# Local attention of a two-layer block: values as zero-padded blocks, one multiply out of PSUM, gating by inverse sums on GpSimd

## The chip, the core and the metric

The kernel runs on one core of a Trainium2 chip. The metric is the time of one execution on the device in microseconds (us). Five queues of instructions run side by side: TensorE (PE, with its weight loads shown as PEld), VectorE (DVE), ScalarE (ACT), GpSimd (POOL) and the DMA issues of SyncE (SP). Each works through its own program in order; they meet at semaphores.

## The reference, cut to what matters

The whole program is two blocks: an even mixer, an odd mixer, and a second block with a gated feed-forward part. The change lies in the odd mixer, an attention over a window of keys with a sink, 1024 tokens, 16 query heads in 4 groups of 4 that share one key and value head, head size 64:

```python
def windowed_sink_attention(q, k, v, sink, slopes):
    ...                                   # a block of 128 queries sees its own 128 keys and those on either side
    sc = jnp.einsum('bnqkgd,bnskd->bnkgqs', qb, kb).astype(jnp.float32) * scale + bias
    m = jnp.maximum(jnp.max(sc, axis=-1, keepdims=True), sink_l)
    p = jnp.exp(sc - m)
    denom = jnp.sum(p, axis=-1, keepdims=True) + jnp.exp(sink_l - m)
    o = jnp.einsum('bnkgqs,bnskd->bnqkgd', (p / denom).astype(v.dtype), vb)

def odd_mixer(h, w_in, sink, w_out, slopes):
    qc, kc, vc, gc = jnp.split(h @ w_in, [C_Q, C_Q + C_KV, C_Q + 2 * C_KV], axis=-1)
    oc = windowed_sink_attention(...)
    return (oc * jax.nn.silu(gc)) @ w_out
```

Products are made from two rounded parts of each operand, a high one and a low one (the rest after rounding), so that a product takes three matrix products: high by high, low by high, high by low.

## The kernel before, in words

The odd mixer is three stages: projection (`*_odd_proj`), the local attention (`*_attention_c`), output projection (`*_odd_out`). The attention walks over 32 groups g, each one key head i = g // 8 and one block of 128 queries n = g % 8. A group has four query heads and is done as two units u = 2g and u = 2g + 1 of two heads each. A block sees three blocks of keys, at the two ends of the sequence (n = 0 and n = 7) two.

Each engine has a loop over u written by hand, and the order in it is the order of execution. In the step of unit u:

- PE: scores of u (`pe_c_scores`, six matmuls into PSUM banks 0 and 1, in pairs on two halves of the array); transposes of the exponentials of u - 1 (`pe_c_turn`, two or three for each head); in odd steps `pe_c_spread`, two transposes of the inverse sums into bank 7; in even steps `pe_c_values` of group u / 2 - 2 into bank 6.
- DVE: `dve_c_bias` twice (adds the bias to the scores out of PSUM and takes the row's extreme), `dve_c_low` of u - 2 (the low part of the transposed exponentials); in even steps the inverse of the sums first, and `dve_c_gate` last; in odd steps `dve_c_add` last.
- ACT: `act_c_raise` twice (exponentials with their sums), `act_c_high` of u - 1 (the high part out of PSUM); in even steps `act_c_move`. In steps 5, 7 and 9 of each key head but the last it also makes the high parts of the next head's keys (`act_c_keys`) and queries (`act_c_query`).
- POOL: in even steps `pool_c_wide` (spreads the inverse sums over 64 columns for a head), in odd steps `pool_c_mix`, and in between the low parts of the next head's keys, queries and values and its bias tables. `c_pool_in_turn` makes every POOL operation wait for the one before it.

Scores of unit u wait for the biases of u - 1, since banks 0 and 1 are there once. Transposes of u - 1 wait for the exponentials of u - 1 (`c_raised`) and for the low parts of u - 3 (`c_low`), which free their banks. The values of a group wait for its low parts and for the last reader of bank 6 in the group before.

Before, the weights of the value product are 128 columns, 64 of the high part of V and 64 of its low part (`C_VS`), and the moving operand is all four heads, 512 columns, once with the high exponentials (`C_PTH`) and once with the low ones (`C_PTL`): 2 matmuls for each block of keys, 4 or 6 for a group. Bank 6 then holds two sums in its two halves of 64 rows. ACT moves the lower half to the upper rows (`C_OT`), DVE adds the two in two pieces of 64 x 256 (`C_O2`), and POOL multiplies by `C_G`. That was made by DVE from bank 7 (the inverse sums, transposed) and the gate in `MIX`. The product goes back into `MIX`, which the output projection reads.

Of the kernel before, what the change touches and what calls it, by code (L numbers as in the profile page):

```python
# [14 lines left out]
P = 128  # L15
# [107 lines left out]
def build(nc, d, where, known):  # L123
# [1401 lines left out]
    def act_odd_proj():  # L1525
# [42 lines left out]
    def dve_odd_proj():  # L1568
# [57 lines left out]
    c_biased, c_low, c_inverse, c_gated, c_added, c_key_low0, c_query_low0, c_sinks = signal("c_dve").steps(
        "biased", "low", "inverse", "gated", "added", "key_low0", "query_low0", "sinks")
    c_raised, c_high, c_moved, c_key_high, c_query_high, c_sink = signal("c_act").steps(
        "raised", "high", "moved", "key_high", "query_high", "sink")
# [56 lines left out]
    def pe_c_values(g):  # L1686
# [61 lines left out]
    def dve_c_gate(g):  # L1748
        i, n = g // TT, g % TT
        dve.wait_ge(*c_spread.at(g))  # L1750
        if g >= 2:
            dve.wait_ge(*c_mixed.at(g - 2))
        dve.tensor_tensor(C_G[:, g % 2, :].rearrange("p (t n) -> p t n", t=2),
                          ps[:, 7, 0:2 * P].rearrange("p (t n) -> p t n", t=2), mix_pair(i, n),
                          ALU.mult).then_inc(*c_gated.up(g))

    def dve_c_add(g):
        dve.wait_ge(*c_moved.at(g))
        if g >= 2:
            dve.wait_ge(*c_mixed.at(g - 2))  # L1760
        for e in range(2):
            high, low = (x.rearrange("p (t e n) -> p e t n", t=2, e=2)[:, e]
                         for x in (ps[0:HD, 6, :], C_OT[0:HD, :]))
            last = dve.tensor_tensor(C_O2[g % 2][rows(e, HD), :].rearrange("p (t n) -> p t n", t=2), high, low, ALU.add)
        last.then_inc(*c_added.up(g))
# [16 lines left out]
    def act_c_keys(i):  # L1782
        base = (i % 2) * HD
        for r in range(2):
            act.activation(C_KH[rows(r, HD), i, :], KC[base:base + HD, i // 2, :], ACT.Copy).then_inc(*c_key_high.up(i, r))

    def act_c_query(t):
        if t >= 4:
            act.wait_ge(*c_scored.at(2 * (8 * (t // 2 - 2) + 7) + t % 2, 1))
        else:  # L1790
            act.wait_ge(*vc_turned.at(1))
# [25 lines left out]
    def act_c_move(g):  # L1817
        act.wait_ge(*c_summed.at(g))
        act.activation(C_OT[0:HD, :], ps[HD:P, 6, :], ACT.Copy).then_inc(*c_moved.up(g))

    def act_attention_c():
        act.wait_ge(*w_used.at(ODD_PROJ[-1]))
        for u in range(NU + 5):
# [10 lines left out]
            i = u // 16 + 1  # L1834
            if i < C_KV:
                if u % 16 == 5:
                    act_c_keys(i)
                elif u % 16 in (7, 9):
                    act_c_query(2 * i + (u % 16 - 7) // 2)
            elif u % 16 == 5 and u < NU:  # L1840
                act_high(ODD_OUT[0])

    def pool_c_values(i):
        v = C_VS[:, i % 2, :, :]
# [3 lines left out]
        pool.tensor_copy(v[:, :, 0:HD], VC[:, :, rows(i, HD)]).then_inc(*c_v_high.up(i))  # L1848
# [1245 lines left out]
```

## Time and profile before

| | us |
|---|---|
| median of 3 runs (2415.68 to 2421.56) | 2418.89 |
| the profiled execution | 2413.29 |
| its span, from first to last instruction | 2412.0 |

| engine | busy us | share of the span |
|---|---|---|
| PE | 2322.6 | 96% |
| PEld | 1925.3 | 80% |
| DVE | 1394.3 | 58% |
| ACT | 1133.5 | 47% |
| POOL | 929.8 | 39% |

The local attention takes the time from 1060 to 1237 us of the span, 7% of it. Shares over the whole span tell nothing of this stage, in which other engines do far more than on average; it has to be read by its own window. PE's busy time counts each matmul up to its modelled end, so that a stage with PE 90% busy can still hold waits and overlaps: for PE the starts of instructions are the better guide.

### The profile page before, as it was taken

Reading aid. Unit: us, or ns where it says so; the run is one execution under the profiler, and the core shown is the slowest. Engines: PE = TensorE matmul, PEld = TensorE weight load, DVE = VectorE, ACT = ScalarE, POOL = GpSimd, SP = SyncE. Lnnn points to the kernel's source line nnn. Section 1 sums busy time; section 2 is a strip of 40 time slices with the busy share of each in tenths; the row PEclk is TensorE's granted clock in tenths of the full one; section 3 lists DMA queues with packets and bytes.
Section 4 is the critical chain, followed back from the end, with each engine's and each line's share of the span. In section 5 each row is a group of like instructions: output and inputs, shape, how many; then the busy total and the mean of one; then the engine's idle time right before and its main releaser. Section 6 shows DMA issues by size and latency. Waiting matters only on the chain.

```text
span 2412.0 us, 31494 instructions
## 1 busy us (share of the span) xinstructions
PE 2322.6 (96%) x12074; PEld 1925.3 (80%) x12074; DVE 1394.3 (58%) x1899; ACT 1133.5 (47%) x1796; POOL 929.8 (39%) x711
## 2 busy tenths in 40 slices
PE   5999999989999999998999999999999999999998
PEld 5888789868888888876678777788877888888887
DVE  6256599768884330139973743332676666666665
ACT  5322488778883221249952474232333333333334
POOL 1112256436652212335521112122265555555551
PEclk8999999999999999999999999999999999999999
DMA  8265200010003121100021121122211111111111
GB/s 307 76 166 177 76 6 1 4 33 1 1 1 122 67 95 44 53 1 1 10 105 44 60 95 44 36 83 66 71 31 52 55 55 54 53 53 53 53 53 70
DMA packets 154089, 146.46 MB, mean 61 GB/s; under 512 B 12294, under 2 KB 141364, under 8 KB 152020
## 3 DMA queue, kind: packets, MB, share of 16 engines
q1 hardware_dynamic: 153940, 144.45, 19.2%
q8 instruction: 96, 1.57, 0.3%
q14 instruction: 53, 0.43, 0.1%
HBM read 123.85 MB, written 16.78 MB: 58 GB/s over the span
## 4 chain that ended last, share of the span: by engine, by line
PE 80%; ACT 6%; issue 5%; DVE 4%; POOL 2%; DMA 1%; SPq 1%; ACTq 0%; DVEq 0%; POOLq 0%
PE ps L256 37%; PE ps L2650 15%; PE ps L2667 9%; PE ps L1127 5%; PE ps L1150 4%; PE ps L1137 4%; ACT C_PR L1807 1%; PE ps L1696 1%; POOL WSL L2567 1%; ACT B_PR L1211 1%; ACT B_PTH L1205 1%; PE ps L2626 1%; ACT C_PTH L1815 1%; PE ps L1675 1%; POOL WSR L2549 1%
## 5 line engine op out<-in xcount | busy, mean ns | idle before, releaser
L243 POOL TENSOR_TENSOR WL<-WR,WH 128x1024 fp32r<-128x1024 f32 (+2 forms) x87 | 203.0, 2334 | 764.8 <-ACT WH L238 764.6
L256 PE MATMUL ps<-HH,WH 128*128 128x512 f32 (+2 forms) x1136 | 358.8, 397 | 0.0
L256 PE MATMUL ps<-HL,WH 128*128 128x512 f32 (+2 forms) x1136 | 351.7, 391 | 0.0
L256 PE MATMUL ps<-HH,WL 128*128 128x512 f32 x1104 | 341.8, 391 | 0.0
L256 PEld LDWEIGHTS ps<-HL,WH 128*128 128x128 f32 (+2 forms) x1136 | 212.1, 187 | 47.7
L256 PEld LDWEIGHTS ps<-HH,WH 128*128 128x128 f32 (+2 forms) x1136 | 208.4, 187 | 47.1 <-issue 4.1
L256 PEld LDWEIGHTS ps<-HH,WL 128*128 128x128 f32 x1104 | 208.1, 188 | 44.0
L2880 DVE TENSOR_TENSOR XF<-ps,XF 128x1024 f32<-128x1024 f32 x168 | 201.5, 1220 | 33.0 <-PE ps L2667 26.4
L2650 PE MATMUL ps<-HC,WSH 128*128 128x512 f32 x640 | 197.0, 389 | 0.0
L1163 DVE TENSOR_REDUCE NM<-ps 128x1 f32<-128x1024 f32 x128 | 156.6, 1223 | 35.9 <-PE ps L1127 34.4
L2567 POOL TENSOR_TENSOR WSL<-WSR,WSH 128x512 fp32r<-128x512 f32 x100 | 131.5, 1315 | 107.5 <-ACT WSH L2561 107.5
L2561 ACT ACTIVATE WSH<-WSR 128x512 fp32r<-128x512 f32 x100 | 62.9, 629 | 220.2 <-POOL WSR L2549 220.2
L2549 POOL TENSOR_TENSOR WSR<-WS 128x512 f32<-128x512 f32 x100 | 133.9, 1339 | 36.3 <-PE ps L2650 36.3
L2650 PE MATMUL ps<-HS,WSH 128*128 128x512 f32 x480 | 147.7, 389 | 0.0
L2650 PEld LDWEIGHTS ps<-HC,WSH 128*128 128x128 f32 x640 | 120.1, 188 | 24.9
L2650 PE MATMUL ps<-HC,WSL 128*128 128x512 f32 x320 | 124.6, 389 | 0.0
L2667 PE MATMUL ps<-AH,OWH 128*128 128x512 f32 x352 | 110.0, 394 | 6.5 <-DVE XF L2880 4.4
L2567 POOL TENSOR_TENSOR WSL<-WS,WSH 128x512 fp32r<-128x512 f32 x48 | 65.0, 1356 | 125.7 <-ACT WSH L2561 125.7
L2839 DVE TENSOR_TENSOR CG<-CG,ps 128x512 f32<-128x512 f32 x60 | 41.3, 688 | 119.2 <-ACT CG L2728 89.4
L2667 PE MATMUL ps<-AH,OWL 128*128 128x512 f32 x352 | 108.7, 390 | 0.0
L2667 PE MATMUL ps<-AL,OWH 128*128 128x512 f32 x352 | 108.6, 390 | 0.0
L1726 DVE CUSTOM_DVE_ANT_0 C_SB<-ps,BF,NSINK 128x384 f32<-128x384 f32 (+1 forms) x128 | 68.9, 576 | 67.1 <-POOL C_VS L1848 60.3
(433 smaller groups left out, 5183.0 us busy)
## 6 DMA issues: line engine op xcount, KB each, us to landing
WS<-in_w_ffn_in SPq DMA_DIRECT2D x44, 512.0 KB, 5.0
MKW<-in_ada_w SPq DMA_DIRECT2D x32, 512.0 KB, 3.9
spill<-X SPq DMA_DIRECT2D x3, 4096.0 KB, 13.6
OW<-in_w_ffn_out SPq DMA_DIRECT2D x22, 512.0 KB, 3.5
WR<-in_odd_w_in SPq DMA_DIRECT2D x19, 512.0 KB, 3.7
WR<-in_w_in SPq DMA_DIRECT2D x19, 512.0 KB, 3.7
WR<-in_even_w_in SPq DMA_DIRECT2D x17, 512.0 KB, 5.5
AWK<-in_ada_w SPq DMA_DIRECT2D x8, 1024.0 KB, 9.4
```

The lines of the kernel that those rows point to most:

```text
L243: pool.tensor_tensor(low[:, :, :], raw[:, :, :], high[:, :, :].bitcast(F32), ALU.subtract).then_inc(*w_low.up(t))
L256: last = pe.matmul(ps[0:w.out, 2 * s + h, :], wt[:, k, :], x[:, k, halves(h)], start=(k == 0 and n == 0), stop=(k == w.kt - 1 and n == len ...
L1127: last = pe.matmul(ps[:, b + j, :], qs[:, rows(q)], ks[:, halves(j)], start=(n == 0), stop=(n == len(passes) - 1))
L1137: last = pe.transpose(ps[:, 4 + j, rows(k)], D.PR[:, p % 3, rows(4 * j + k)], IDENT[:, :])
L1150: last = pe.matmul(ps[:, 6 + pg % 2, 0:2 * P], D.VS[D.v_of(h)][:, k, :], pt[pg % 2][:, k, :], start=(k == 0 and n == 0), stop=(k == TT - 1 ...
L1163: dve.tensor_reduce(NM[:, s % 4:s % 4 + 1], pair(2 * (s % 2)), AX_X, ALU.max, negate=True).then_inc(*m_done.up(g, s))
L1726: dve.tensor_tensor_reduce(C_SB[:, hd, WIN - w:WIN], ps[:, j, 0:w], BF[i % 2][:, hd, b0:b0 + w], -1.0, NSINK[:, 4 * i + hd:4 * i + hd + 1] ...
L2549: pool.tensor_tensor(WSR[:, q % RING, :, :], w_block(*a), w_block(*b), op).then_inc(*ws_sum.up(q))
L2567: pool.tensor_tensor(WSL[:, q % RING, :, :], src, WSH[:, q % RING, :, :].bitcast(F32), ALU.subtract).then_inc(*ws_low.up(q))
L2650: last = pe.matmul(ps[:, BANK[o], :], w[:, q % RING, k, :], OPERAND[o][:, x, k, :], start=(k == 0 and n == 0), stop=(k == HK - 1 and n == 2))
L2667: done = pe.matmul(ps[:, 4 + 2 * (n % 2) + h, :], w[:, rows(n)], x[:, halves(h)], start=(first and m == 0), stop=(last and m == 2))
L2880: dve.tensor_tensor(LAST.x[:, n, :], pair(4 + 2 * (n % 2)), LAST.x[:, n, :], ALU.add).then_inc(*y_added.up(r, n))
```

## The change

The value product writes its result where it is wanted. `C_VS` becomes five blocks of 64 columns for each block of keys: zero, V high, zero, V low, zero. A slice of 128 columns that starts at a zero block puts its product in one half of the rows and zeros in the other; two such slices (e = 0 and 1) put the two heads of a pair into the two halves of bank 6. There are three terms (high by high, low by high, high by low) with two slices each, of 256 columns: 6 matmuls for each block of keys, 12 or 18 for a group. `C_PTH` and `C_PTL` hold the heads in another order for this.

With that the move of a half (`C_OT`) and the two additions are gone. ACT copies the transposed inverse sums from bank 7 to `C_G` instead (`act_c_move`), POOL multiplies them there by the gate in `MIX` (`pool_c_gate`), and DVE multiplies bank 6 by `C_G` into `MIX` (`dve_c_mix`). The high parts of the next head's keys and queries go from ACT to POOL (`pool_c_next_keys`, `pool_c_next_query`), and POOL clears the zero blocks (`pool_c_clear`: buffer 0 at the start, buffer 1 in step 5). The output projection waits for `c_mixed` instead of `c_added`.

```diff
     def pe_c_spread(g):
         pe.wait_ge(*c_wide.at(g))
         if g:
-            pe.wait_ge(*c_gated.at(g - 1))
+            pe.wait_ge(*c_moved.at(g - 1))
...
         if g:
-            pe.wait_ge(*c_added.at(g - 1))
-        for k in range(hi - lo):
-            for m, pt in enumerate((C_PTH, C_PTL)):
-                last = pe.matmul(ps[:, 6, :], C_VS[:, i % 2, lo + k, :], pt[:, g % 2, k, :, :].rearrange("p h n -> p (h n)"),
-                                 start=(k == 0 and m == 0), stop=(k == hi - lo - 1 and m == 1))
+            pe.wait_ge(*c_mixed.at(g - 1))
+        v = C_VS[i % 2][:, :, :, :].rearrange("p t b n -> p t (b n)")
+        nk = hi - lo
+        for k in range(nk):
+            for m, (c0, pt) in enumerate(((0, C_PTH), (2, C_PTH), (0, C_PTL))):
+                for e in range(2):
+                    a = HD * (c0 + 1 - e)
+                    last = pe.matmul(ps[:, 6, 0:2 * P], v[:, lo + k, a:a + P], pt[:, g % 2, k, e, :, :].rearrange("p t n -> p (t n)"),
+                                     start=(k == 0 and m == 0 and e == 0), stop=(k == nk - 1 and m == 2 and e == 1))
...
-    def dve_c_gate(g):
...
-    def dve_c_add(g):
...
+    def dve_c_mix(g):
         i, n = g // TT, g % TT
+        dve.wait_ge(*c_gated.at(g))
+        dve.wait_ge(*c_summed.at(g))
+        dve.tensor_tensor(mix_pair(i, n), ps[:, 6, 0:2 * P].rearrange("p (t n) -> p t n", t=2),
+                          C_G[:, g % 2, :].rearrange("p (t n) -> p t n", t=2), ALU.mult).then_inc(*c_mixed.up(g))
...
-            if u % 2 == 0 and 4 <= u < NU + 4:
-                dve_c_gate((u - 4) // 2)
             if u % 2 == 1 and 5 <= u < NU + 5:
-                dve_c_add((u - 5) // 2)
+                dve_c_mix((u - 5) // 2)
...
     def act_c_move(g):
-        act.wait_ge(*c_summed.at(g))
-        act.activation(C_OT[0:HD, :], ps[HD:P, 6, :], ACT.Copy).then_inc(*c_moved.up(g))
+        act.wait_ge(*c_spread.at(g))
+        if g >= 2:
+            act.wait_ge(*c_mixed.at(g - 2))
+        act.activation(C_G[:, g % 2, :], ps[:, 7, 0:2 * P], ACT.Copy).then_inc(*c_moved.up(g))
...
-            i = u // 16 + 1
-            if i < C_KV:
-                if u % 16 == 5:
-                    act_c_keys(i)
-                elif u % 16 in (7, 9):
-                    act_c_query(2 * i + (u % 16 - 7) // 2)
...
+    def pool_c_clear(b):
+        for block in (0, 2, 4):
+            c_pool_in_turn()
+            pool.memset(C_VS[b][:, :, block, :].bitcast(F32), 0.0).then_inc(*c_v_clear.up(b, block))
...
+    def pool_c_next_keys(i):
+        base = (i % 2) * HD
+        for r in range(2):
+            c_pool_in_turn()
+            pool.tensor_copy(C_KH[rows(r, HD), i, :], KC[base:base + HD, i // 2, :]).then_inc(*c_next_key.up(i, r))
+
+    def pool_c_next_query(t):
+        if t >= 4:
+            pool.wait_ge(*c_scored.at(2 * (8 * (t // 2 - 2) + 7) + t % 2, 1))
+        c_pool_in_turn()
+        pool.tensor_copy(C_QH[t % 4][:, :], QC[:, t, :]).then_inc(*c_next_query.up(t))
...
-    def pool_c_mix(g):
+    def pool_c_gate(g):
...
+        g_ = C_G[:, g % 2, :].rearrange("p (t n) -> p t n", t=2)
+        pool.tensor_tensor(g_, g_, mix_pair(i, n), ALU.mult).then_inc(*c_gated.up(g))
...
             if u % 2 == 0 and 2 <= u <= NU:
                 pool_c_wide((u - 2) // 2)
-            if u % 2 == 1 and 5 <= u < NU + 5:
-                pool_c_mix((u - 5) // 2)
+            if u % 2 == 0 and 4 <= u < NU + 4:
+                pool_c_gate((u - 4) // 2)
+            if u == 5:
+                pool_c_clear(1)
...
+                elif u % 16 == 5:
+                    pool_c_next_keys(i)
                 elif u % 16 == 6:
                     pool_c_keys(i)
+                elif u % 16 in (7, 9):
+                    pool_c_next_query(2 * i + (u % 16 - 7) // 2)
...
     def pe_odd_out():
         pe_stay_awake(7, 0)
-        pe.wait_ge(*c_added.at(NG - 1))
+        pe.wait_ge(*c_mixed.at(NG - 1))
```

On PE, in an even step of a middle block, this is what stood between the scores of one unit and those of the next (L1662 scores, L1675 transposes, L1696 values):

```order
L1662 MATMUL ps<-C_KL_180,C_QH_184 128x384 x2
L1675 MATMUL ps<-IDENT,C_PR 128x128 x6
L1696 MATMUL ps<-C_PTH,C_VS 128x512
L1696 MATMUL ps<-C_PTL,C_VS 128x512
L1696 MATMUL ps<-C_PTH,C_VS 128x512
L1696 MATMUL ps<-C_PTL,C_VS 128x512
L1696 MATMUL ps<-C_PTH,C_VS 128x512
L1696 MATMUL ps<-C_PTL,C_VS 128x512
L1662 MATMUL ps<-C_KH,C_QH_185 128x384 x2
```

The same place on PE in the changed kernel (its lines are 1661, 1674 and 1699):

```order
L1661 MATMUL ps<-C_KL_180,C_QH_184 128x384 x2
L1674 MATMUL ps<-IDENT,C_PR 128x128 x6
L1699 MATMUL ps<-C_PTH,C_VS_188 128x256 x4
L1699 MATMUL ps<-C_PTL,C_VS_188 128x256 x2
L1699 MATMUL ps<-C_PTH,C_VS_188 128x256 x4
L1699 MATMUL ps<-C_PTL,C_VS_188 128x256 x2
L1699 MATMUL ps<-C_PTH,C_VS_188 128x256 x4
L1699 MATMUL ps<-C_PTL,C_VS_188 128x256 x2
L1661 MATMUL ps<-C_KH,C_QH_185 128x384 x2
```

Nothing moved on PE: the value product stands where it stood, with 18 matmuls of 256 columns for 6 of 512.

On POOL, in steps 4 to 10 of the first key head, the order before (L1857 bias table, L1887 mix, L1879 wide, L1865 low part of keys, L1871 of queries):

```order
L1857 TENSOR_SCALAR BF_200<-AWAY,SLOPE 128x384
L1887 TENSOR_TENSOR MIX<-C_O_194,C_G 128x2x128
L1879 COPY C_RID<-C_RI 128x256
L1865 TENSOR_TENSOR C_KL_181<-KC,C_KH 64x1024 x2
L1887 TENSOR_TENSOR MIX<-C_O_195,C_G 128x2x128
L1879 COPY C_RID<-C_RI 128x256
L1871 TENSOR_TENSOR C_QL<-QC,C_QH_186 128x1024
L1887 TENSOR_TENSOR MIX<-C_O_194,C_G 128x2x128
L1879 COPY C_RID<-C_RI 128x256
L1871 TENSOR_TENSOR C_QL<-QC,C_QH_187 128x1024
```

The same steps on POOL in the changed kernel (L1883 gate, L1827 clear, L1857 and L1863 the copies that came from ACT):

```order
L1843 TENSOR_SCALAR BF_198<-AWAY,SLOPE 128x384
L1827 MEMSET C_VS_189 128x8x64 x3
L1857 CAST C_KH<-KC 64x1024 x2
L1875 COPY C_RID<-C_RI 128x256
L1883 TENSOR_TENSOR C_G<-C_G,MIX 128x256
L1850 TENSOR_TENSOR C_KL_181<-KC,C_KH 64x1024 x2
L1863 CAST C_QH_186<-QC 128x1024
L1875 COPY C_RID<-C_RI 128x256
L1883 TENSOR_TENSOR C_G<-C_G,MIX 128x256
L1867 TENSOR_TENSOR C_QL<-QC,C_QH_186 128x1024
L1863 CAST C_QH_187<-QC 128x1024
L1875 COPY C_RID<-C_RI 128x256
```

The copies stand ahead of the wide steps, and the multiply by the gate has moved from behind the additions of the odd step to the even step, right behind the wide step of the next group.

## Rows read from the trace of the kernel before

**Rows 1.** Busy time in the local attention's window: PE, PEld, DVE, ACT, POOL, clock, DMA

```profile
1060.00:1237.00 177.00, 156.67 (x1009) 112.81 (x1008) 159.51 (x449) 158.53 (x374) 89.87 (x97) 1.00 0.02 6
```

**Rows 2.** Timeline of one group: start, length, engine, line, operation, idle before and releaser

```profile
1208.68 0.45 PE L1662 MATMUL ps<-C_KH,C_QH 64*128 64x384 f32 x2
...
1209.51 0.62 DVE L1726 CUSTOM_DVE_ANT_0 C_SB<-ps,BF,NSINK 128x384 f32<-128x384 f32 x1 [0.23 <-PE ps L1662]
...
1210.43 0.48 PEld L1662 LDWEIGHTS ps<-C_KH,C_QH 64*128 64x128 f32 x2 [0.17 <-issue]
...
1210.59 0.95 DVE L1740 TENSOR_TENSOR C_PTL<-ps,C_PTH 128x768 fp32r<-128x768 f32 x1
...
1211.66 0.64 PEld L1675 LDWEIGHTS ps<-IDENT,C_PR 128*128 128x128 f32 x6 [0.46 <-ACT C_PR L1807]
...
1212.44 0.47 PE L1696 MATMUL ps<-C_PTH,C_VS 128*128 128x512 f32 x1
...
1213.66 0.39 PE L1696 MATMUL ps<-C_PTL,C_VS 128*128 128x512 f32 x1
...
1213.97 0.44 PE L1662 MATMUL ps<-C_KH,C_QH 64*128 64x384 f32 x2
```

**Rows 3.** Groups by shape in the same window: count, busy us, mean ns, idle before

```profile
L1696 PE MATMUL ps<-C_PTH,C_VS 128*128 128x512 f32 x88 | 37.0, 421 | 2.1 <-DVE C_O L1764 1.4
```

**Rows 4.** Timeline of an earlier attention's value product, eight matmuls of 256 columns

```profile
395.76 0.36 PE L1150 MATMUL ps<-A_PTH,A_VS 128*128 128x256 f32 x1
...
395.96 0.28 PE L1150 MATMUL ps<-A_PTL,A_VS 128*128 128x256 f32 x1
...
396.68 0.28 PE L1150 MATMUL ps<-A_PTL,A_VS 128*128 128x256 f32 x1
```

**Rows 5.** Timeline of PE: first scores of five odd units

```profile
1118.54 0.44 PE L1662 MATMUL ps<-C_KH,C_QH 64*128 64x384 f32 x2
...
1136.23 0.45 PE L1662 MATMUL ps<-C_KH,C_QH 64*128 64x384 f32 x2
...
1160.78 0.44 PE L1662 MATMUL ps<-C_KH,C_QH 64*128 64x384 f32 x2
...
1178.62 0.44 PE L1662 MATMUL ps<-C_KH,C_QH 64*128 64x384 f32 x2
...
1224.60 0.39 PE L1662 MATMUL ps<-C_KH,C_QH 64*128 64x256 f32 x2
```

**Rows 6.** Groups by shape, as Rows 3: what is removed, added or moved

```profile
L1764 DVE TENSOR_TENSOR C_O<-ps,C_OT 64x256 f32<-64x256 f32 x64 | 26.4, 412 | 2.7 <-ACT C_OT L1819 2.2
L1819 ACT ACTIVATE C_OT<-ps 64x512 f32<-64x512 f32 x32 | 19.0, 595 | 4.1 <-PE ps L1696 3.4
L1887 POOL TENSOR_TENSOR MIX<-C_O,C_G 128x256 f32<-128x256 f32 x24 | 17.7, 739 | 44.6 <-DVE C_O L1764 44.2
L1871 POOL TENSOR_TENSOR C_QL<-QC,C_QH 128x1024 fp32r<-128x1024 f32 x6 | 14.3, 2388 | 1.2 <-ACT C_PR L1807 0.4
L1879 POOL COPY C_RID<-C_RI 128x256 f32<-128x256 f32 x32 | 12.8, 398 | 7.6 <-POOL MIX L1887 3.2 <-DVE C_RI L1746 2.8 <-POOL GATE L1887 0.9
L1753 DVE TENSOR_TENSOR C_G<-ps,MIX 128x256 f32<-128x256 f32 x24 | 10.0, 415 | 0.0
L1792 ACT ACTIVATE C_QH<-QC 128x1024 fp32r<-128x1024 f32 x6 | 6.3, 1053 | 0.0
L1848 POOL CAST C_VS<-VC 128x512 fp32r<-128x512 f32 x4 | 2.5, 616 | 17.7 <-PE ps L256 17.4
```

**Rows 7.** Waits in the same window: who waited for whom, us, times, longest

```profile
PEld ps L1696 <- DVE C_O L1764: 3.8, 8, 1.6
```

**Rows 8.** Timeline of the attention's end

```profile
1231.21 0.47 PE L1696 MATMUL ps<-C_PTH,C_VS 128*128 128x512 f32 x1 [1.44 <-DVE C_O L1764]
...
1232.41 0.59 ACT L1819 ACTIVATE C_OT<-ps 64x512 f32<-64x512 f32 x1 [2.23 <-PE ps L1696]
...
1234.72 3.90 ACT L435 ACTIVATE HH<-MIX 128x1024 fp32r<-128x1024 f32 x4 [1.72 <-POOL GATE L1887]
```

More of the change, by code:

```diff
@@ L1620, in build @@
-    C_OT, C_O2 = place("C_OT", 139.53125, [P, HALF]), [place("C_O20", 141.53125, [P, 2 * P]), place("C_O21", 117.75, [P, 2 * P])]
+    C_KL = [place(f"C_KL{i}", kb, [P, SEQ], F32R) for i, kb in enumerate((107.5, 149.5, 153.5, 157.5))]
+    C_QH = [place(f"C_QH{i}", kb, [P, SEQ], F32R) for i, kb in enumerate((51, 55, 161.5, 165.5))]
+    C_VS = [place("C_VS0", 117.5, [P, TT, 5, HD], F32R), place("C_VS1", 169.5, [P, TT, 5, HD], F32R)]
+    C_PTH, C_PTL = place("C_PTH", 179.5, [P, 2, 3, 2, 2, P], F32R), place("C_PTL", 191.5, [P, 2, 3, 2, 2, P], F32R)
@@ L1624, in build @@
     c_tables = signal("c_tables")
     c_scored, c_turned, c_spread, c_summed = signal("c_scored"), signal("c_turned"), signal("c_spread"), signal("c_summed")
[L1626 to L1629, printed above, removed]
+    c_biased, c_low, c_inverse, c_mixed, c_key_low0, c_query_low0, c_sinks = signal("c_dve").steps(
+        "biased", "low", "inverse", "mixed", "key_low0", "query_low0", "sinks")
@@ L1630, in build @@
+    c_raised, c_high, c_key_high, c_query_high, c_sink, c_moved = signal("c_act").steps(
+        "raised", "high", "key_high", "query_high", "sink", "moved")
     c_pool = signal("c_pool")
-    c_mixed, c_wide, c_bias, c_v_high, c_values, c_key_low, c_query_low = c_pool.steps(
-        "mixed", "wide", "bias", "v_high", "values", "key_low", "query_low")
+    c_wide, c_gated, c_bias, c_v_clear, c_v_high, c_values, c_next_key, c_next_query, c_key_low, c_query_low = c_pool.steps(
+        "wide", "gated", "bias", "v_clear", "v_high", "values", "next_key", "next_query", "key_low", "query_low")
@@ L1746, in dve_c_inverse @@
         dve.reciprocal(C_RI[:, g % 2, :], C_RS[:, g % 2, :]).then_inc(*c_inverse.up(g))
-    def dve_c_gate(g):
+    def dve_c_mix(g):
         i, n = g // TT, g % TT
[L1750 to L1755, printed above, removed]
-    def dve_c_add(g):
[L1758 to L1765, printed above, removed]
+        dve.wait_ge(*c_gated.at(g))
+        dve.wait_ge(*c_summed.at(g))
+        dve.tensor_tensor(mix_pair(i, n), ps[:, 6, 0:2 * P].rearrange("p (t n) -> p t n", t=2),
+                          C_G[:, g % 2, :].rearrange("p (t n) -> p t n", t=2), ALU.mult).then_inc(*c_mixed.up(g))
     def dve_attention_c():
@@ L1776, in dve_attention_c, with act_c_keys @@
                 dve_c_low(u - 2)
-            if u % 2 == 0 and 4 <= u < NU + 4:
-                dve_c_gate((u - 4) // 2)
             if u % 2 == 1 and 5 <= u < NU + 5:
-                dve_c_add((u - 5) // 2)
-    def act_c_keys(i):
-        base = (i % 2) * HD
+                dve_c_mix((u - 5) // 2)
+    def act_c_keys():
         for r in range(2):
-            act.activation(C_KH[rows(r, HD), i, :], KC[base:base + HD, i // 2, :], ACT.Copy).then_inc(*c_key_high.up(i, r))
+            act.activation(C_KH[rows(r, HD), 0, :], KC[0:HD, 0, :], ACT.Copy).then_inc(*c_key_high.up(0, r))
     def act_c_query(t):
[L1788 to L1791, printed above, removed]
+        act.wait_ge(*vc_turned.at(1))
         act.activation(C_QH[t % 4][:, :], QC[:, t, :], ACT.Copy).then_inc(*c_query_high.up(t))
@@ L1847, in pool_c_values @@
         c_pool_in_turn()
[L1848 removed]
+        pool.tensor_copy(v[:, :, 1, :], VC[:, :, rows(i, HD)]).then_inc(*c_v_high.up(i))
         c_pool_in_turn()
[L1850 removed]
+        pool.tensor_tensor(v[:, :, 3, :], VC[:, :, rows(i, HD)], v[:, :, 1, :].bitcast(F32),
                            ALU.subtract).then_inc(*c_values.up(i))
@@ L1880, in pool_c_wide @@
                          C_RI[:, g % 2, :].unsqueeze(2).to_broadcast([P, 4, HD])).then_inc(*c_wide.up(g))
-    def pool_c_mix(g):
+    def pool_c_gate(g):
         i, n = g // TT, g % TT
-        mix = mix_pair(i, n)
-        pool.wait_ge(*c_added.at(g))
+        pool.wait_ge(*c_moved.at(g))
         c_pool_in_turn()
-        pool.tensor_tensor(mix, C_O2[g % 2][:, :].rearrange("p (t n) -> p t n", t=2),
-                           C_G[:, g % 2, :].rearrange("p (t n) -> p t n", t=2), ALU.mult).then_inc(*c_mixed.up(g))
+        g_ = C_G[:, g % 2, :].rearrange("p (t n) -> p t n", t=2)
+        pool.tensor_tensor(g_, g_, mix_pair(i, n), ALU.mult).then_inc(*c_gated.up(g))
     def pool_attention_c():
```

20 lines of the change are left out of this document (7 added, 13 removed).

## The prediction

> **What bounds the kernel now.** The change touches one stage, so I read that stage by its own window first. There three engines stand level: of 177 us PE is busy for 156.7, DVE for 159.5, ACT for 158.5, POOL for half of that, and the granted clock is 1.00, the level of 2.4 GHz [rows 1]. Busy shares so close together don't say which engine sets the pace; a loop of waits can. So the next view is the timeline of one group in the middle of a key head, and the reader is to follow from the scores of one odd unit to the scores of the next odd unit [rows 2]:
>
> - Scores start at 1208.68. DVE had been idle for 0.23 when they released its first bias at 1209.51: it follows the scores and isn't late. The two biases end where the low part begins, 1210.59.
> - The transposes of that unit need its exponentials (ACT, behind the biases) and the low part that stands behind the biases on DVE, 1210.59 + 0.95 = 1211.54. They start at 1211.66, after PE's loads had been idle for 0.46 [rows 2]. From the scores that is 2.98.
> - Transposes take up to 1212.44, 0.78. Then the value product, six matmuls, the last at 1213.66; the next odd scores follow it at 1213.97, 1.53 after the first.
>
> 2.98 + 0.78 + 1.53 = 5.29, and that is the measured distance of the two odd scores. So the pace is a loop through PE, DVE, ACT and PE again, in which **the value product stands in line** with the two biases and the low part. The additions, the gate multiply and the move are not in it: they run while the loop is elsewhere. Three such periods in an undisturbed stretch are 1224.60 - 1208.68 = 15.92, 5.31 each [rows 2, 5].
>
> I take the sum against the profiled execution, 2413.29 (span 2412.0 and 1.3 around it). It lies 5.6 below the median of the runs, 2418.89, and the forecast is the median plus the change.
>
> **The change part by part.**
>
> *The value product, in the loop.* 88 blocks of keys (88 matmuls with the high part [rows 3], as many with the low) have 2 matmuls of 512 columns each and get 6 of 256. In the middle of a product the starts of 512-column matmuls lie (1213.66 - 1212.44) / 5 = 0.244 apart with the first one's delay, about 0.229 without it (the first takes some 0.08 more, as 0.20 against 0.12 in [rows 4]). For 256 columns with 128 x 128 weights the trace has the same form in an earlier attention, with a new weight load each time: 395.96 to 396.68 are six steps of 0.12 [rows 4]. A group of three key blocks goes from 6 x 0.229 = 1.37 to 18 x 0.12 = 2.16, **+0.79**; one of two blocks from 0.92 to 1.44, **+0.52**. There are 24 of the one and 8 of the other: 24 x 0.79 + 8 x 0.52 = **+23.1**. Nothing covers it, since the next scores wait in PE's queue behind it and the biases wait for them.
>
> The Trainium skill, "TensorE: Matmul & The Clock Gate", section "Back-to-back issue gap", gives a warm gap of N / 2.4 + 2.5 ns. By it 256 columns would take 0.109 and 512 take 0.216, and the term would be an estimated 24 x 0.67 + 8 x 0.45 = 19.7 instead of 23.1. The rows show a little more for both widths, and I keep the rows.
>
> *Additions, gate, mix on DVE.* Two additions of 0.412 go for each group, and one multiply out of PSUM replaces another of the same shape (0.415) [rows 6]. DVE loses 64 x 0.412 = 26.4 busy us, but in the loop it works only at the biases and the low part, which stay: worth nothing there. Only where PE has fewer transposes (four instead of six) do the additions come late for the next values. Seven such waits are left of [rows 7] beside the one of 1.6 at the end: 2.2 together, with the usual gap of a load in it; **-1.5**. The new multiply stands behind the same low part, 0.415 instead of 0.82 long, and doesn't wait there: its gate was made a group before.
>
> *ACT's move.* 64 x 512 (0.595) becomes 128 x 256, half the columns; between nothing and 0.595 a group, off the loop. It now waits for the spread instead of the sum, and the next exponentials queue behind it; the spread stands one step earlier on PE, so I cost it at nothing. If it did hold ACT, its slack before the next transposes is the long value product.
>
> *Keys and queries from ACT to POOL.* Four ACT operations of some 1.05 a head [rows 6] go from steps 5 to 9. What they cost now is read from odd scores three periods apart: 1136.23 - 1118.54 = 17.69 and 1178.62 - 1160.78 = 17.84 [rows 5] against 15.92. That is 1.77 and 1.92; the first head is taken like these: 3 x 1.84 = **-5.5**.
>
> On POOL they are new work. A copy with rounding takes 0.616 for 512 columns, so 1.23 for 1024; the other bound is the two-operand form with 2.39 [rows 6]. I take 1.23, the same operation. Between the wide steps of groups 2 and 3 of a head POOL then has 0.40 + 0.74 + 2 x 2.39 + 1.23 = 7.15, and five gaps between operations of up to 0.24 (7.6 idle ahead of 32 wide steps [rows 6]), so 7.2 to 8.4, against a new period of 5.30 + 0.79 = 6.09. The spread on PE can be late by 0 to 2.3 a head, in the first head by three clears of 0.40 to 0.62 more (copy and cast [rows 6] as bounds): 0 to 8.8 in all. Most is absorbed, since the inverse sums are ready nearly a period before the spread stands at the head of PE's queue: half a microsecond a head, **+1.5**.
>
> *The end.* There is no cover there. PE waited 1.44 for the last additions but one [rows 8]; without move and additions, 0.595 + 0.82, but with a multiply of 0.415, it waits 1.0 less. From the last sums to the output projection's first operation on ACT were 1234.72 - 1232.41 = 2.31 [rows 8], move, additions and POOL's 0.74; a multiply of 0.415 and a hand-over remain, about 0.5: 1.8 less. **-2.8**. The waits of output projection and its loads hang on `c_mixed` before and after, and shift with it.
>
> Sum: 23.1 - 1.5 - 5.5 + 1.5 - 2.8 = **+14.8**: 2413.29 becomes 2428.1, and the median 2418.89 becomes **2433.7**.
>
> **The rivals.**
>
> *The relieved engines set the pace (not slower).* If the waits in the loop went away with the lighter DVE and ACT, only PE's own work would count. Of the 5.29 PE waited 0.46 ahead of the transposes and about 0.29 ahead of the second even scores (a pair of loads that takes 0.48 and not 0.19 [rows 2]). 5.29 - 0.75 + 0.79 = 5.33 a period, as much as now, and what remains are the -1.5, -5.5 and -2.8: 2418.89 - 9.8 + 32 x 0.03 = 2410. It decides from the point where the first bias no longer starts with the scores' end. For it speaks DVE's 90% [rows 1]; against it the 0.23 in which DVE stood idle for the scores. The Trainium skill, "Perfetto Trace Analysis", section "Optimizing Scalar/DVE Operations", says that offloading a saturated DVE to ScalarE or GpSimd may make sense; by that rule this is the likely case, and the idle time in the loop is what the trace says against it. Chance 0.10.
>
> *POOL becomes the bound in steps 5 to 10 (slower still).* There it has three times 0.40 + 0.74, four copies of 1.23 and four low parts of 2.39, 17.9, with 14 gaps up to 21.3, in three periods of 6.09 = 18.3; up to 3.0 too much, which its lead absorbs. Were the copies at the two-operand price, 4 x 1.16 = 4.6 more, a head would lose up to 7.6 and three heads 23 instead of the 1.5: +36 at most, 2455. Against it: the cast in this stage's rows is cheap [rows 6]. Chance 0.12, mostly in part of that size.
>
> *The value product is hidden after all.* PE's waits could lie elsewhere in other groups, so that the longer product fills them; with 0.46 of each 0.79 hidden the sum is +14.8 - 32 x 0.44 = about +1, 2420. Against it: the wait ahead of the transposes starts at the odd scores, which move with the product. Chance 0.08.
>
> **How the numbers follow.** The forecast has 0.70, its own range 2427 to 2441 (skill's gaps below; POOL's term at 8.8 above). The range for 8 in 10 takes in most of the third case and the nearer half of the POOL case: 2420 to 2446. Within 0.2%, 4.8 us, a measurement of this kernel can't tell a change from none. Slower: 0.70 + 0.12 and little of the rest, 0.82. Faster: 0.09 of the first rival. Same: 0.09.
>
> **What would show it.** Right: 256-column value matmuls 0.12 apart; odd scores 6.1 apart in the middle of a head where it was 5.3; DVE near 159.5 - 26.4 = 133 busy us in the stage and ACT near 140 (158.5 less twelve operations of 1.05 and part of the move), both with idle time; PE's wait ahead of the transposes still there, released by ACT or the low part; the last sums within 0.6 of the output projection. Wrong: odd scores 5.3 to 5.4 apart (first rival); PE's scores or transposes waiting for POOL's spread, or DVE's multiply for POOL's gate, by over a microsecond a head (second); a transposes' wait shrunk to nothing (third).

## The result and the profile after

The changed kernel takes 2427.29 us in the median against 2420.22 of the kernel before beside it, a ratio of 1.0035 with an interval of 1.0024 to 1.0046: 6 to 11 us slower, where +14.8 was forecast (2433.7, range 2420 to 2446). Direction and range hold; the forecast change is half as large again as the +9.7 that the stage shows (next paragraph) and lies above the interval.

The stage, from its first scores to the first matmul of the output projection, was 177.0 (1060.15 to 1237.16) and is 186.7 (1067.03 to 1253.69): **+9.7**. The profiled run began it 6.9 later, after a wait for weights some 800 us earlier and a stretch at a granted clock of 0.50 (6.8 us) right behind that wait, which the change doesn't touch, and was 2.9 shorter behind the stage; I compare within the stage. Busy time there, with the columns of [rows 1]:

```profile
1067.00:1253.70 186.70, 175.47 (x1362) 146.24 (x1361) 133.90 (x386) 136.50 (x362) 105.33 (x115) 1.00 0.02 7
```

DVE has lost 26 us of work and ACT 22, as meant, and the stage is longer: PE's busy time has gone up by 19. One group of the timeline answers to [rows 2]:

```profile
1218.94 0.44 PE L1661 MATMUL ps<-C_KH,C_QH 64*128 64x384 f32 x2
...
1219.77 0.62 DVE L1729 CUSTOM_DVE_ANT_0 C_SB<-ps,BF,NSINK 128x384 f32<-128x384 f32 x1 [1.56 <-PE ps L1661]
...
1221.72 0.41 DVE L1755 TENSOR_TENSOR GATE<-ps,C_G 128x256 f32<-128x256 f32 x1
1221.92 0.64 PEld L1674 LDWEIGHTS ps<-IDENT,C_PR 128*128 128x128 f32 x6 [0.46 <-ACT C_PR L1792]
...
1222.55 0.72 PE L1699 MATMUL ps<-C_PTH,C_VS 128*128 128x256 f32 x4
...
1223.35 0.64 PE L1699 MATMUL ps<-C_PTH,C_VS 128*128 128x256 f32 x4
...
1224.07 0.64 PE L1699 MATMUL ps<-C_PTH,C_VS 128*128 128x256 f32 x4
...
1224.88 0.44 PE L1661 MATMUL ps<-C_KH,C_QH 64*128 64x384 f32 x2
```

Odd scores to odd scores: 5.94, where it was 5.29. Scores to transposes is 2.98 as before, with the same 0.46 of waiting for the exponentials. The product takes 2.33 for 1.53 (1223.35 to 1224.07 is six matmuls, 0.12 each). Between them stand 0.63 from transposes to product, where 0.78 stood. DVE waits 1.56 for the scores instead of 0.23: it idles longer in a longer loop.

What was added and moved, by shape as [rows 6]: DVE's multiply, ACT's copy, POOL's gate, wide step and one of the copies.

```profile
L1755 DVE TENSOR_TENSOR MIX<-ps,C_G 128x256 f32<-128x256 f32 x24 | 10.0, 415 | 1.4 <-POOL C_G L1883 1.4
L1806 ACT ACTIVATE C_G<-ps 128x256 f32<-128x256 f32 x32 | 11.8, 368 | 1.5 <-PE ps L1682 1.5
L1883 POOL TENSOR_TENSOR C_G<-C_G,MIX 128x256 f32<-128x256 f32 x24 | 17.6, 732 | 29.2 <-ACT C_G L1806 27.9 <-POOL C_RID L1875 0.4
L1875 POOL COPY C_RID<-C_RI 128x256 f32<-128x256 f32 x32 | 12.7, 398 | 26.8 <-DVE C_RI L1749 24.4 <-POOL C_QH L1863 0.8 <-POOL C_KH L1857 0.5
L1863 POOL CAST C_QH<-QC 128x1024 fp32r<-128x1024 f32 x6 | 6.2, 1038 | 0.7
```

The new waits are nearly all idle time of engines off the loop. The end, to be read against [rows 8]:

```profile
1249.97 0.40 PE L1699 MATMUL ps<-C_PTL,C_VS 128*128 128x256 f32 x2
1250.21 3.73 PE L368 MATMUL ps<-IDENT 128*128 128x128 f32 x32
1250.47 0.42 DVE L1755 TENSOR_TENSOR GATE<-ps,C_G 128x256 f32<-128x256 f32 x1 [1.92 <-PE ps L1699]
...
1250.93 5.79 ACT L435 ACTIVATE HH<-MIX 128x1024 fp32r<-128x1024 f32 x6 [2.27 <-DVE GATE L1755]
...
1253.69 0.70 PE L256 MATMUL ps<-HH,ODD_FIRST 128*128 128x512 f32 x2
```

One multiply stands between the last sums and the output projection's first operation: 0.56 from the modelled end of the sums (1249.97 + 0.40 = 1250.37) to 1250.93, where 2.31 stood. What comes last there now is PE's own filler (L368, matmuls without a use with which `pe_stay_awake` fills the wait; 1253.69 follows them without a gap).

### The profile page after: what moved, and what is told of

Read it like the earlier page. It is cut to its first block, busy times and chain, and to the rows that moved or that the text cites. A ratio compares the mean times of both kernels' runs of the same rounds, so it can differ in the third digit from the quotient of the medians.

```text
span 2425.6 us, 32135 instructions
## 1 busy us (share of the span) xinstructions
PE 2342.9 (97%) x12426; PEld 1959.5 (81%) x12426; DVE 1367.1 (56%) x1835; ACT 1110.3 (46%) x1784; POOL 947.0 (39%) x729
## 4 chain that ended last, share of the span: by engine, by line
PE 82%; DVE 5%; ACT 4%; issue 4%; POOL 2%; DMA 2%; SPq 1%; DVEq 0%; ACTq 0%; POOLq 0%
PE ps L256 35%; PE ps L2652 15%; PE ps L2669 9%; PE ps L1127 5%; PE ps L1150 4%; PE ps L1137 4%; PE ps L1699 2%; DMA MKW<-in_ada_w 1%; PE ps L1661 1%; PE ps L1674 1%; ACT B_PR L1211 1%; ACT B_PTH L1205 1%; PE ps L2628 1%; DMA WR<-in_w_in 1%; DVE MKA L525 1%
```

## The experiments

Theory: the pace is the loop of [rows 2], and the product stands in line. Open were where 5 us of the forecast went, and what ACT's relief is worth in a shorter loop. A period is the time from the scores of one odd unit to those of the next. Besides the ratio to the kernel before I give the time from the third odd scores (unit 5) to the first matmul of the output projection, since in most of the profiled runs (not in before, after and e1) PE's clock fell at the start of the stage. Windows of e14_before_spread (columns as [rows 1]):

```profile
1066.00:1071.50 5.50, 3.18 (x26) 2.13 (x24) 2.42 (x10) 4.95 (x12) 4.72 (x6) 0.99 0.00 0
1071.50:1077.50 6.00, 6.00 (x26) 4.30 (x25) 3.98 (x14) 3.84 (x11) 3.91 (x4) 0.50 0.01 4
```

After a stretch in which PE was busy for 3.18 of 5.5, the granted clock was 0.50 (1.2 GHz) for 6 us; that costs about 2.4 us ahead of the third odd scores (13.3 from the first scores to them, 10.9 in before).

| kernel | ratio to before, 95% | third odd scores to output projection, us |
|---|---|---|
| before | 1 | 166.1 |
| after | 1.0035 [1.0024, 1.0046] | 175.3 |
| e13_before_one_addition | 0.9966 [0.9953, 0.9978] | 160.7 |
| e2_mix_halves | 1.0072 [1.0055, 1.0089] | 181.6 |
| e1_two_terms | 0.9979 [0.9967, 0.9991] | 164.3 |
| e3_copies_on_act | 1.0042 [1.0026, 1.0058] | 176.0 |
| e6_clear_later | 1.0034 [1.0023, 1.0045] | 173.8 |
| e5_before_pool_copies | 1.0032 [1.0022, 1.0041] | 171.9 |
| e14_before_spread | 0.9970 [0.9959, 0.9981] | 161.6 |
| e9_before_split | 1.0102 [1.0084, 1.0120] | 188.4 |
| e8_split_product | 1.0009 [1.0000, 1.0019] | 167.8 |
| e10_split_clear | 1.0000 [0.9990, 1.0010] | 165.4 |
| e11_split_act_copies | 1.0016 [1.0003, 1.0029] | 167.1 |
| e12_split_spread | 0.9983 [0.9973, 0.9993] | 160.8 |

**What did the additions cost?** First the changed kernel with its multiply as slow as the two additions:

```diff
+        for e in range(2):
+            r = rows(e, HD)
+            last = dve.tensor_tensor(mix_pair(i, n)[r], ps[r, 6, 0:2 * P].rearrange("p (t n) -> p t n", t=2),
+                                     C_G[r, g % 2, :].rearrange("p (t n) -> p t n", t=2), ALU.mult)
+        last.then_inc(*c_mixed.up(g))
```

> The changed kernel with VectorE's multiply in two pieces of 64 rows, as long (0.83) as the two additions that it replaced and in the same place. Theory A: in the kernel before, the next product waited for the additions in every group (0.15 in the middle, 0.36 where four transposes stand ahead), and the change took that wait away; then it comes back here: 24 x 0.15 + 8 x 0.36 = 6.5 us slower than the changed kernel, transposes to product 0.78 again instead of 0.63. Rival B: the forecast's 1.5 for this wait was right and the forecast was off elsewhere; then +1 to +2 us.

It is 6.3 longer from the third odd scores on, 0.9 of it at the end, behind the last odd scores: the theory's size. Then the kernel before with one addition fewer:

```diff
-        for e in range(2):
+        for e in range(2 if g < 2 else 1):
```

> The kernel before, with the second of the two additions of a group left out from the third group on (so heads' odd halves of the result aren't brought up to date: that part of the computation is missing). The additions' end then comes 0.42 us earlier, and nothing else of the product or of ScalarE changes. In the trace of before the product began 0.14 to 0.15 us after the second addition's end in 18 of 32 groups, and there it stood 0.75 us behind its transposes with six of them and 0.67 to 0.72 with four, against 0.63 and about 0.4 in the changed kernel. Theory (the additions held the product in these groups, and the loop of odd scores passes through that): 11 x 0.12 + 3 x 0.33 + 4 x 0.26 = 3.4 us less in the stage (177.0 to 173.6), middle odd scores of the last head 5.15 to 5.2 instead of 5.29 to 5.32, time about 3.5 below before (ratio 0.9985). Rival (the prediction's size): 1.5 us less, odd scores at 5.29, ratio 0.9994.

It is 5.4 shorter by the same measure, 1.2 of it at the end, which the expectation had left out; middle odd scores of the last head lie 5.17 to 5.18 apart, as the theory said, those around a change of heads 4.52, 3.85 and 4.65 where they were 4.88, 4.15 and 4.91. DVE's last operation on the sums, from the timelines, in before (its product starts at 1212.44 [rows 2]), e2 and e13:

```profile
1211.46 0.83 DVE L1764 TENSOR_TENSOR C_O<-ps,C_OT 64x256 f32<-64x256 f32 x2
```

```profile
1228.11 0.85 DVE L1757 TENSOR_TENSOR GATE<-ps,C_G 64x256 f32<-64x256 f32 x2
...
1229.11 0.59 PE L1699 MATMUL ps<-C_PTH,C_VS 128*128 128x256 f32 x3
```

```profile
1216.03 0.41 DVE L1764 TENSOR_TENSOR C_O<-ps,C_OT 64x256 f32<-64x256 f32 x1
...
1216.86 0.47 PE L1696 MATMUL ps<-C_PTH,C_VS 128*128 128x512 f32 x1
```

From DVE's end to the product: 0.15 in before and e2, 0.42 in e13 and in after (1221.72 + 0.41 to 1222.55). Over all groups it is 0.14 to 0.15 in 18 of 32 before, 0.14 to 0.16 in nearly every group of e2, and in after 0.19 or more but for the last group. So a constant 0.15 marks the groups in which the product waited for DVE. Most of these waits carry no label [rows 7]: the modelled end of the transposes lies behind the product's start there, so that PE shows no idle time.

**Does the product set the period?** After without the term of V's low part, 12 matmuls instead of 18:

```diff
-            for m, (c0, pt) in enumerate(((0, C_PTH), (2, C_PTH), (0, C_PTL))):
+            for m, (c0, pt) in enumerate(((0, C_PTH), (0, C_PTL))):
...
```

> The changed kernel without one of the three terms of the value product (low part of V by high exponentials is left out): 12 matmuls of 256 columns in a middle group instead of 18. Theory: the product stands in the loop that sets the pace, so each of the 88 key blocks gives back 4 x 0.12 = 0.24 x... worked out: two matmuls of 0.12 less for each key block, 88 x 0.24 = 21 us, unless the loop becomes so short (5.93 - 0.72 = 5.2) that another engine holds it; 2406, and odd scores 5.2 apart in the middle of a head. Rival (the changed kernel is held by GpSimd's longer work): odd scores stay near 5.9, time within 5 us of 2427.

Middle odd scores lie 5.21 apart, 0.72 less, six matmuls of 0.12. But only half of the gain arrives (11.0 of 21): in heads 0 to 2 single periods of 10.35, 8.27 and 6.76 appear, PE's transposes of the inverse sums waiting for POOL:

```profile
PEld ps L1682 <- POOL C_RID L1875: 9.0, 5, 3.1
```

The two longest are not POOL's alone: in them the granted clock is 0.50, for 6.8 us from the end of the wait on and for 3.4 us right behind it. In the longest the product of 12 matmuls takes 2.84; it takes 1.60 otherwise.

**What are the copies on ACT worth?** In the changed kernel, put back:

```diff
...
+                if u % 16 == 5:
+                    act_c_next_keys(i)
+                elif u % 16 in (7, 9):
+                    act_c_query(2 * i + (u % 16 - 7) // 2)
...
```

> The changed kernel with the high parts of the next keys and queries on ScalarE again, as before. If their move is worth what odd scores showed (5.5 us before), this is 5.5 - 1.5 = 4 us slower than the changed kernel, odd scores 6.5 or more apart in steps 5 to 7. Rival: in the longer loop ScalarE has the time for them, and only GpSimd's delay in the first head (1.5 us) goes: -1.5 to +2 us.

Two periods in each of heads 0 to 2 are longer than 5.93: 6.10 to 6.23, and 6.31 (6.62 in head 0). That is 0.55 to 0.97 a head and 2.2 in all. The one late period of after, worth 1.5, is gone, so that 0.7 remains, and the time is that of after: in the long loop ACT has room for most of the copies, and the move was worth next to nothing. In the kernel before, moved to POOL at the steps where the change puts them:

```diff
+                elif u % 16 == 5:
+                    pool_c_next_keys(i)
...
+                elif u % 16 in (7, 9):
+                    pool_c_next_query(2 * i + (u % 16 - 7) // 2)
...
```

> The kernel before with one part of the change alone: the high parts of the next keys and queries made by GpSimd instead of ScalarE. Theory: 5.5 us less (odd scores 5.3 apart throughout), less what GpSimd's later spread costs in the shorter period: 2415 to 2419. Rival: GpSimd becomes the bound in steps 5 to 10, no gain or a loss.

The rival came: ACT's 1.8 a head is gone, the middle odd scores lie 5.3 to 5.5 apart, but for one period of 8.8 to 8.95 in each of heads 0 to 2. POOL's timeline there:

```profile
1125.89 2.14 POOL L1865 CAST C_KH<-KC 64x1024 fp32r<-64x1024 f32 x2
1128.18 0.40 POOL L1883 COPY C_RID<-C_RI 128x256 f32<-128x256 f32 x1 [0.16 <-DVE C_NM L1726]
1128.66 4.85 POOL L1858 TENSOR_TENSOR C_KL<-KC,C_KH 64x1024 fp32r<-64x1024 f32 x2
1133.66 0.73 POOL L1891 TENSOR_TENSOR MIX<-C_O,C_G 128x256 f32<-128x256 f32 x1
1134.52 1.03 POOL L1871 CAST C_QH<-QC 128x1024 fp32r<-128x1024 f32 x1
1135.71 0.40 POOL L1883 COPY C_RID<-C_RI 128x256 f32<-128x256 f32 x1 [0.16 <-DVE C_O L1764]
```

From one wide step (L1883) to the next are 7.53, with gaps of 0.16 at most, in a loop of 5.3. That makes PE 2.2 late, and the period is 3.6 longer. The rest is the clock. PE's wait for POOL, the product behind it and the next odd scores, and the window of the product, in which the granted clock is 0.50 (columns as [rows 1]):

```profile
1136.17 0.44 PE L1683 MATMUL ps<-IDENT,C_RID 128*128 128x128 f32 x2 [2.55 <-POOL C_RID L1883]
...
1138.10 0.78 PE L1696 MATMUL ps<-C_PTH,C_VS 128*128 128x512 f32 x1
...
1140.93 0.50 PE L1662 MATMUL ps<-C_KH,C_QH 64*128 64x384 f32 x2
```

```profile
1137.70:1141.10 3.40, 3.40 (x12) 2.36 (x11) 2.02 (x6) 2.06 (x6) 2.97 (x4) 0.50 0.00 0
```

The product takes 2.83 instead of 1.56, and the same fall of 3.4 us stands in each of the three heads. A late engine thus cost PE twice here: the wait of 2.2, and 1.4 at half the clock behind it. So the same work, spread over the head:

```diff
...
+                elif u % 16 in (0, 5):
+                    pool_c_next_keys(i, u % 16 // 5)
+                elif u % 16 in (6, 8):
+                    pool_c_keys(i, u % 16 // 2 - 3)
+                elif u % 16 in (9, 12):
+                    pool_c_next_query(2 * i + u % 16 // 12)
+                elif u % 16 in (10, 13):
+                    pool_c_query(2 * i + u % 16 // 13)
+                elif u % 16 == 14:
+                    pool_c_values(i)
```

> e5_before_pool_copies (the kernel before with the copies of keys and queries on GpSimd) with GpSimd's preparation of the next head spread over steps 0, 5, 6, 8, 9, 10, 12, 13 and 14 as in e12_split_spread: tells whether the relief of ScalarE alone, without the product of zero-padded blocks, would have made the kernel faster. Theory (only the bunching made GpSimd late there): no period above 5.5 in heads 1 and 2, the 1.8 us a head that the copies cost are gone, stage 177.0 - 5.4 = 171.6 to 172, time about 5 below before (ratio 0.998), level with e12_split_spread. Rival (before has no room on GpSimd: its product with the inverse sums waits in an odd step for the additions, and what comes behind it is late for the next spread): one or two periods of 6 to 7 a head remain, stage 176 to 179, ratio 1.000 or above.

All middle periods are 5.31 to 5.33, but for one of 5.49 in the last head, in which ACT also rounds weights of the output projection. At a change of heads 0.2 is lost, and no fall of the clock is left but the one at the start. 4.6 are gained where 5.0 to 5.4 were expected, and the kernel is faster than before: 0.9970. In the short loop the copies' move is worth 4.6, in the long one 0.7, or 2.2 once the clear is out of the way (next).

**The clear.** After with the zeros of the second buffer written at step 11 instead of 5:

```diff
-            if u == 5:
+            if u == 11:
```

> The changed kernel with the clearing of the second buffer of V moved from step 5 to step 11, behind the copies of keys and queries. In the changed kernel the spread of one group in the first head waits 2.1 us for GpSimd, and odd scores there lie 7.5 apart instead of 5.9. Theory: these 1.5 us go, and nothing else changes: 1 to 2 us faster than the changed kernel. Rival: the wait comes from the copies, not from the clear, and stays.

The one late period of after (7.46 in head 0) is 5.93, and 1.5 are gone from the third odd scores on; the time can't tell it from after.

**Can the product leave the line?** The last key block's six matmuls moved to the end of the odd step:

```diff
-        for k in range(nk):
+        for k in ([nk - 1] if last_block else range(nk - 1)):
...
+            if u % 2 == 1 and 5 <= u:
+                pe_c_values((u - 5) // 2, True)
...
```

> The changed kernel with the same instructions, but the last key block's six matmuls of each value product moved from the even step to the end of the following odd step, where TensorE waits for biases. Theory (a loop through the even step's product sets the pace): 0.72 leaves the loop in each of 32 groups, odd scores 5.2 apart in the middle of a head instead of 5.93, 32 x 0.72 = 23 us less at most, 2404 to 2410, faster than the kernel before. Rival (TensorE's own work is the bound): nothing is gained by moving work on the same engine, 2427 within 3 us.

The middle odd scores lie 5.40 apart, not 5.2, and POOL is late once a head (7.1, in head 0 7.8). With the same instructions on PE it is 7.5 shorter than after from the third odd scores on, of 23 at most, and not faster than before. The gain came another way than the expectation had it. From odd scores to the even ones behind them it is 2.46 where after has 1.74: the moved 0.72 in full, since PE had no wait there to fill. From even scores to the next odd ones it is 2.95 for 4.19: 0.72 of the product, and 0.52 of PE's wait ahead of the transposes, which is gone. The same split in the kernel before:

> The kernel before with the last key block's two matmuls moved from the even to the odd step, as in e8_split_product. Theory: VectorE, with the additions, has 5.15 of work in a period of 5.30, so the loop can be shortened by 0.15 only: 0 to 4 us less, or a loss where move and additions come a step closer to the next product. If so, the gain in e8_split_product rests on the work that the change took from VectorE and ScalarE. Rival: 0.46 x 32 = 15 us less here too.

It is 22 us longer, where 0 to 4 less were expected, or a loss by another way (move and additions closer to the next product). Waits of e9 and, for the same transposes, of before:

```profile
PE ps L1675 <- ACT C_PR L1811: 45.1, 41, 1.8
ACT C_OT L1823 <- PE ps L1697: 37.0, 32, 2.2
```

```profile
PE ps L1675 <- ACT C_PR L1807: 11.6, 21, 1.5
```

The later sums hold ACT's move (37.0 of idle time, 4.1 in before [rows 6]), the exponentials stand behind it in ACT's queue, and PE waits for those. The change took that move away. That this is what lets the product be split is read from these waits; no run moved ACT's move alone.

**The split with POOL and ACT.** The edits are those shown above, put together: e8's split with e6's clear (e10); that with e3's copies on ACT (e11); and the split with POOL's work spread as in e14, the clear at step 14 (e12).

> As e8_split_product, with the clearing of the second buffer of V in step 11 instead of 5. Theory: in the shorter loop GpSimd's delay in the first head costs at least the 1.5 us it costs in the changed kernel; 1.5 to 3 us faster than e8_split_product. Rival: GpSimd is late by the copies alone, no difference.

> e10_split_clear with the copies of the next head's keys and queries back on ScalarE (four of 1.05 us a head), as in the kernel before. ScalarE's own work in a period of the split loop is four exponentials of 0.61 + 0.19, two moves of 0.79 and one of 0.37 = 5.15 us of 5.40. Theory (with the split ScalarE is as good as full, so that here, unlike with the unsplit product, the move off ScalarE is what pays): each copy adds about 0.8 us to its period, 3.2 a head and 9.6 in all, against 4.8 that GpSimd no longer costs: stage about 183, time about 2422. Rival (ScalarE absorbs them as in e3_copies_on_act, 0.55 us a head): stage 178.5 - 4.8 + 1.7 = 175.4, time about 2414.

> Changed kernel with the product split as in e8_split_product, and GpSimd's preparation of the next head (two key copies, two key low parts, two query copies, two query low parts, the value blocks) spread over steps 0, 5, 6, 8, 9, 10, 12, 13 and 14 of a head instead of 5 to 10 and 12; every instruction is the same. In e10_split_clear the odd scores stood 5.40 us apart but for one period of about 7.0 in each of three heads, behind GpSimd's spread-out inverse sums. Theory (GpSimd was late only because its extra work of 2.4 to 4.9 us is bunched): no period above 5.6, three times 1.6 us gone, stage 178.5 - 4.8 = 173.7 us, time 2417.3 - 4.8 = 2412.5, which is some 0.2 per cent faster than the kernel before. Rival (GpSimd has no room in a period of 5.40: its own copies and gates take 1.13 plus waits of about 3): three or four periods a head at 5.7 to 6.3 in place of one at 7.0, stage 177 to 178.5 and no gain.

PE's waits of e10, in which a period of about 7.0 a head stayed, and all of e12's:

```profile
PE ps L1682 <- POOL C_RID L1879: 4.2, 3, 1.5
```

```profile
PE ps L1674 <- ACT C_PR L1796: 1.5, 1, 1.5
PE ps L1661 <- DVE C_NM L1733: 0.8, 1, 0.8
PE ps L1700 <- DVE GATE L1759: 0.7, 1, 0.7
PE ps L1674 <- DVE C_PTL L1747: 0.4, 1, 0.4
```

In e12 POOL holds no transposes of the sums any more, 4.6 of the expected 4.8 are gone against e10, and at 2413.91 it is a little faster than before (2415.97 beside it; the interval leaves out 1), no more than e14 is without the blocks. e11 came out between theory and rival in the stage (180.2): two periods of 6.4 to 6.7 a head, so ACT has too little room for the copies at 5.40. What holds the middle periods at 5.41 in e12 is PE's own work:

```profile
1217.62 0.44 PE L1661 MATMUL ps<-C_KH,C_QH 64*128 64x384 f32 x2
...
1218.35 0.87 PE L1674 MATMUL ps<-IDENT,C_PR 128*128 128x128 f32 x6
1218.97 0.71 PE L1700 MATMUL ps<-C_PTH,C_VS 128*128 128x256 f32 x4
...
1220.57 0.44 PE L1661 MATMUL ps<-C_KH,C_QH 64*128 64x384 f32 x2
...
1221.29 0.88 PE L1674 MATMUL ps<-IDENT,C_PR 128*128 128x128 f32 x6
1222.00 0.38 PE L1682 MATMUL ps<-IDENT,C_RID 128*128 128x128 f32 x2
1222.14 0.72 PE L1700 MATMUL ps<-C_PTH,C_VS 128*128 128x256 f32 x4
...
1223.03 0.45 PE L1661 MATMUL ps<-C_KH,C_QH 64*128 64x384 f32 x2
```

Scores 0.73, transposes 0.62, twelve value matmuls 1.60, scores 0.72, transposes 0.71, inverse sums 0.14, six value matmuls 0.89: 5.41, with no wait of PE among them; 0.72 from scores to transposes is the shortest that any run shows. So the unsplit change has 5.41 of PE's work in a period of 5.93, and the split takes out the 0.52 of waiting. For a shorter period PE itself would need less work; no run tried that with the split.

## Why the prediction came out 5 us too high

- **Product, +23.1.** From the product's start to the next scores it is 2.32 in the mean after and 1.56 before with three key blocks (1.53 in the group of [rows 2]), 1.60 and 1.10 with two: 24 x 0.77 + 8 x 0.51 = +22.6. The step holds, and e1 shows that the product is in line. The other estimate, 19.7, was too low. The Trainium skill, "TensorE: Matmul & The Clock Gate", section "Back-to-back issue gap", gives the formula behind it for an isolated matmul. The prediction left that out; here each matmul brings a weight load, and 256 columns take 0.12 and not 0.109.
- **Additions' wait, -1.5: the term that was mis-sized.** The prediction took the waits that [rows 7] labels and said that elsewhere the additions are "worth nothing", since loop time is biases and low part. They ended the product's wait in 18 of 32 groups, also in the very group of [rows 2]: they end at 1211.46 + 0.83 = 1212.29 and the product begins 0.15 later, and of the 0.78 that the prediction gives to the transposes 0.63 is left without them. What the other terms leave of the +9.7 is 9.7 - 22.6 + 5.4 - 1.5 + 2.5 = **-6.5**, with 5.4 for what the three long periods of heads 0 to 2 lie above 5.31 in before. Two runs bear that size out: e2, 6.3 longer with the additions' length put back, and e13, 5.4 shorter without one of them; up to the last odd scores it is 5.4 and 4.2. e13 is the smaller, since ACT still has its copies there and the product waits for the additions in 18 groups; with the copies off ACT (e14) it does in 24. This is a part of the first rival, the relieved engine: its waits of 0.46 ahead of the transposes didn't go, but the one behind them did. So the period is 5.93 and not 6.09.
- **Copies off ACT, -5.5.** Against the short loop right (e14: -4.6, and 0.6 given back by POOL at the changes of heads). But terms don't add freely: against the long loop the copies on ACT cost 2.2, and the move is worth 0.7 (e3).
- **POOL, +1.5.** The size is right, its place isn't: all of it is one period of head 0, with the clears, and e6 takes it away. That the sizes agree is luck. In the 5.93 loop POOL keeps up otherwise; in one of 5.2 to 5.4 it doesn't while its work is bunched (e1, e5, e8), and does once it is spread (e12, e14). The second rival was wrong for this kernel and right one loop shorter, though not by its price: the copies are cheap there too.
- **The end, -2.8.** From the last but one product to the first matmul of the output projection 9.24 became 8.06; without the longer products, 0.77 + 0.51, that is -2.5.
- **Other rows.** DVE 134 (133 forecast) and ACT 137 (140) busy us; the casts on POOL 1.04 (1.23).

That the medians differ by less (+7) than the stage (+9.7) is within the interval.

## What to carry to other kernels

Find the loop before counting busy time: 48 us of work taken off DVE and ACT gave back 14 of the 22.6 us that PE's longer work added in line. Then add up the slowest engine's own work in a turn of the loop: the difference, 0.52 of 5.93 here, is the most that another order of the same work can win in a turn. To learn whether a producer holds a consumer, measure the distance from its end to the start behind it over all groups; a constant smallest distance was a wait here, labelled or not, as e2 and e13 show. Work that is handed to an idle engine has to be spread as finely as the loop turns, and what it is worth depends on how long the loop is.

## What the hardware showed that I had not expected

A rounding copy of 1024 columns takes 1.04 on POOL, the same as on ACT (1.05), while the two-operand form takes 2.39 [rows 6]. ACT's time out of PSUM went with the columns: 0.368 for 128 x 256 and 0.595 for 64 x 512 [rows 6], the same number of elements. The clock's fall at the start of the stage came in most of the profiled runs (in e14 with PE busy for 3.68 of the first 6.0 us of the stage) and not in others of nearly the same PE work (3.56 in before); what decides it stays open. Later in the stage it came in e1 and e5 alone, at or behind the end of waits of PE for POOL of 1.8 to 2.9 us, and not behind another of 1.85 in e1 and one of 2.1 in e8.
